# Two transformer blocks in one kernel: weight loads in another order beside a projection, SBUF tensors at other addresses

## What is computed

```python
# first block
proj = rmsnorm(h) @ w_in                       # q, k, v, gate of 8 retention heads, q, k, v of 8 forgetting heads
h = h + concat(silu(rg) * groupnorm(retention), forgetting_attention) @ w_out
h = h + softmax(q k / 16) v @ w_xo             # q = rmsnorm(h) @ w_xq; k, v from 256 memory rows @ w_xkv
h = h + (silu(hn @ w_gate) * (hn @ w_up)) @ w_down          # 1024 -> 2816 -> 1024
# second block, modulated by a condition c
sh1, sc1, g1, sh2, sc2, g2 = split(silu(c) @ w_ada + b_ada)  # six vectors of 1024
h = rmsnorm(x) * (1 + sc1) + sh1;  x = x + g1 * (concat(attention, pool_mixer) @ w_out)
h2 = rmsnorm(x) * (1 + sc2) + sh2; x = x + g2 * conv_gated_ffn(h2)   # 1024 -> 2 x 2816 -> 1024
```

## The kernel before

| tensors | before |
|---|---|
| h, xh, xl, raw, whi, wlo (every buffer) | 128 |
| tmp, rstd, region: fh, fl, xah, xal, memh, meml, qxh, expd, probt | 64 |
| adar 0 and 1, adacc | 64 |
| adar 2 and 3, adasum (they lie in xh and xl) | 128 |

## Time and profile before

### The profile page before, as it was taken

How to read it: one execution, slowest core, us unless ns; L and a number is a source line. 1 busy time by engine, 2 the same in 40 slices (tenths; PEclk the granted TensorE clock), 3 DMA queues, 4 the chain that set the end, 5 groups by cost and what they waited for, 6 DMA issues and landing times.

```text
span 1446.3 us, 17892 instructions
## 1 busy us (share of the span) xinstructions
PE 1387.2 (96%) x6616; PEld 1106.9 (77%) x6616; DVE 815.7 (56%) x1231; ACT 615.4 (43%) x851; POOL 613.0 (42%) x456
## 2 busy tenths in 40 slices
PE   5999999899989999999999889998999999999999
PEld 3777965788876888888888776874678888888887
DVE  6511957356433577777789994579355554553000
ACT  4634328553344443443441112478435455463111
POOL 4344420274430444445444444331244555556453
PEclk8999999999999999999999998999999999999999
DMA  6123112142220243433445552210121322232322
GB/s 258 59 89 114 58 58 88 41 143 109 88 87 1 88 151 144 156 131 131 147 160 207 206 196 102 88 59 30 59 88 58 109 94 87 92 111 87 117 87 87
DMA packets 28336, 154.19 MB, mean 107 GB/s; under 512 B 2944, under 2 KB 4096, under 8 KB 13952
## 3 DMA queue, kind: packets, MB, share of 16 engines
q1 hardware_dynamic: 28288, 153.52, 29.5%
HBM read 151.41 MB, written 2.10 MB: 106 GB/s over the span
## 4 chain that ended last, share of the span: by engine, by line
issue 42%; PE 30%; POOL 24%; DVE 3%; POOLq 0%; DMA 0%; ACT 0%; SPq 0%
POOL wlo L371 24%; PE lin L1318 10%; PE lin L1320 9%; PE lin L1319 9%; DVE small L984 1%; DVE expd L995 1%; PE lin L1512 0%; PE att L1374 0%; DMA h<-x_t 0%; DVE win L1208 0%; POOL tmp L364 0%; POOLq L365 0%; DVE small L988 0%; PE att L1389 0%; PE att L1383 0%
## 5 line engine op out<-in xcount | busy, mean ns | idle before, releaser
L371 POOL TENSOR_TENSOR wlo<-raw,whi 128x512 fp32r<-128x512 f32 x448 | 608.0, 1388 | 810.4 <-ACT whi L384 535.3
L1318 PE MATMUL lin<-xh,whi 128*128 128x512 f32 x1072 | 423.0, 395 | 4.3 <-POOL wlo L371 3.6
L1320 PE MATMUL lin<-xh,wlo 128*128 128x512 f32 x1072 | 418.1, 390 | 0.0
L1319 PE MATMUL lin<-xl,whi 128*128 128x512 f32 x1072 | 417.8, 390 | 0.0
L1318 PEld LDWEIGHTS lin<-xh,whi 128*128 128x128 f32 x1072 | 201.7, 188 | 51.8 <-issue 6.1
L1320 PEld LDWEIGHTS lin<-xh,wlo 128*128 128x128 f32 x1072 | 201.7, 188 | 42.8
L384 ACT ACTIVATE whi<-raw 128x2048 fp32r<-128x2048 f32 x67 | 128.4, 1917 | 247.8 <-PE lin L1320 211.2
L1319 PEld LDWEIGHTS lin<-xl,whi 128*128 128x128 f32 x1072 | 201.8, 188 | 41.1 <-issue 0.5
L1318 PE MATMUL lin<-fh,whi 128*128 128x512 f32 x352 | 142.2, 404 | 5.5 <-POOL wlo L371 5.5
L1319 PE MATMUL lin<-fl,whi 128*128 128x512 f32 x352 | 141.1, 401 | 0.0
L1320 PE MATMUL lin<-fh,wlo 128*128 128x512 f32 x352 | 140.9, 400 | 0.0
(11 more groups left out here) (292 smaller groups left out, 1961.8 us busy)
## 6 DMA issues: line engine op xcount, KB each, us to landing
raw<-w_slabs SPq DMA_DIRECT2D x112, 1024.0 KB, 4.8
adar<-ada SPq DMA_DIRECT2D x48, 512.0 KB, 3.3
h<-x_t SPq DMA_DIRECT2D x4, 512.0 KB, 7.1
decay<-decay SPq DMA_DIRECT2D x4, 512.0 KB, 8.6
out_t<-h SPq DMA_DIRECT2D x3, 512.0 KB, 8.2
rope<-rope SPq DMA_DIRECT2D x2, 512.0 KB, 8.1
memx<-mem_t SPq DMA_DIRECT2D x1, 1024.0 KB, 5.6
rcnt<-rcnt SPq DMA_DIRECT2D x4, 256.0 KB, 5.0
```

The lines of the kernel that those rows point to most:

```text
L371: last = nc.gpsimd.tensor_tensor(wlo[s][:, ks, :], raw[s][:, ks, :], f(whi[s][:, ks, :]), ALU.subtract)
L1318: nc.tensor.matmul(out, whi_, xhi_, start=first, stop=False)
L1319: nc.tensor.matmul(out, whi_, xlo_, start=False, stop=False)
L1320: return nc.tensor.matmul(out, wlo_, xhi_, start=False, stop=last)
```

## The change

It has two parts. The list in SP's order for the first down projection becomes (2, 3, 3, 3, 3, 3, 3, 2) where it was (4, 3, 3, 3, 3, 3, 2, 1), 22 tiles in both. And the tensors are placed otherwise: par, mod, small, cact, warm and convp come first, then h at the next multiple of 2048 with xh, xl and raw behind it, then the weight buffers with bytes of their own added to them, then rstd, tmp and region, and con between region and tail.

| tensors | after, modulo 256 |
|---|---|
| h, xh, xl, raw (also 0 modulo 2048) | 0 |
| whi 0, whi 1, wlo 0, wlo 1 | 32, 96, 160, 224 |
| rstd, tmp, region: fh, fl, xah, xal, memh, meml, qxh, expd, probt, and con | 0 |
| adar 0 and 1, adacc | 64 |
| adar 2 and 3, adasum | 0 |

```diff
--- before.py
+++ after.py
@@ -103,6 +103,14 @@
             return {n: sem(f"{prefix}_{n}") for n in names.split()}
 
 
+        par = sb("par", [P, PARAMS["end"]])
+        mod = sb("mod", [P, MODS])
+        small = sb("small", [P, 64])
+        cact = sb("cact", [P, KT])
+        warm = sb("warm", [P, 1])
+        convp = [sb(f"convp{i}", [P, 8]) for i in range(2)]
+        at[0] = -(-at[0] // 2048) * 2048
+
         h = sb("h", [P, KT, T])
         xh_at = at[0]
         xh = sb("xh", [P, KT, T], F32R)
@@ -111,20 +119,18 @@
 
         ret_raw = sb("ret_raw", [P, 4, T], offset=xl_at)
         raw = [sb(f"raw{i}", [P, KT, COLS]) for i in range(2)]
-        whi = [sb(f"whi{i}", [P, KT, COLS], F32R) for i in range(2)]
-        wlo = [sb(f"wlo{i}", [P, KT, COLS], F32R) for i in range(2)]
-        par = sb("par", [P, PARAMS["end"]])
-        con = sb("con", [P, CONSTS["end"]])
-        mod = sb("mod", [P, MODS])
-        small = sb("small", [P, 64])
-        cact = sb("cact", [P, KT])
-        warm = sb("warm", [P, 1])
-        convp = [sb(f"convp{i}", [P, 8]) for i in range(2)]
+        wh_at = at[0]
+        at[0] += 4 * 4 * KT * COLS
+        wl_at = wh_at + 2 * 4 * KT * COLS
+        whi = [sb(f"whi{i}", [P, KT, COLS], F32R, offset=wh_at + i * 4 * KT * COLS + (32, 96)[i]) for i in range(2)]
+        wlo = [sb(f"wlo{i}", [P, KT, COLS], F32R, offset=wl_at + i * 4 * KT * COLS + (160, 224)[i]) for i in range(2)]
+        at[0] += 256
         rstd = sb("rstd", [P, T])
         tmp_at = at[0]
         tmp = [sb(f"tmp{i}", [P, T]) for i in range(4)]
         region = at[0]
         at[0] += 88 * 1024
+        con = sb("con", [P, CONSTS["end"]])
         tail = at[0]
 
         def rg_sb(name, shape, kib, dt=F32):
@@ -326,7 +332,7 @@
                 load_ada(j, j - FT)
 
             j = FT + 4
-            for u, more in enumerate((4, 3, 3, 3, 3, 3, 2, 1)):
+            for u, more in enumerate((2, 3, 3, 3, 3, 3, 3, 2)):
                 for _ in range(more):
                     sp.wait_ge(ada["acc"], j - 3)
                     load_ada(j, (j - FT) % 4)
```

## The result

| | before | after |
|---|---|---|
| median of 4 runs, us | 1449.74 | 1463.65 |
| lowest, highest | 1448.65, 1450.37 | 1460.12, 1465.28 |
| the profiled execution | 1448.1 | 1465.28 |
| its span | 1446.3 | 1463.5 |

The ratio is 1.009, with a 95% interval from 1.0076 to 1.0105: 13.9 us slower. The forecast was 1415 us. The time lies in the range, near its upper end, and on the other side of no change.

What follows compares the result with a forecast made beforehand. TensorE's (PE's) matmul steps were taken as the bound; savings of 19.2 (xh), 13.3 (fh, xah) and 2.6 us (mix_tm), 35.1 in sum, took 1448.1 to 1413.0, plus 2.0 for the median: 1415 us. Own range 1402 to 1435, whole 1390 to 1470.

Steps and rivals of the forecast that it cites:

- The reading of the rows: On PE: the next weight load and running stream meet in SBUF, as addresses and relative timing set; 6.7 to 20.0 ns overhead.
- The order edit: First down projection: value 0, ±3.7 us, since VectorE's unbroken chain bounds it; PE's slab 7 gain is lost at the last modulation.
- Rival 5: First down projection: if VectorE's chain weren't the bound, 5.5 us of waits and cold starts would go, some 8 us less; no chance given.
- Addresses outside PE: On VectorE, ScalarE and GpSimd: new addresses cost 0; a tenth more on ScalarE or GpSimd would hide.
- The step that failed: On PE: the smallest overhead in any row, 6.7 ns from memk, taken for all products, 35.1 us less in sum.
- the term of xh: 2880 matmuls with xh as moving operand: step goes to 220.0 ns, 6.67 ns less each, 19.2 us less.
- that of fh and xah: 996 matmuls with fh or xah as moving operand: 13.3 ns less each, 13.3 us less.
- rival 4: 512-column xh products, ffn stages above all: equal residues were the good case, 233.3 ns everywhere, slower, 1468 us; chance 0.21.
- Rival 1: PE's products: the conflict goes altogether, steps of 213.3 ns, 63.4 us less, 1387 us; chance 0.19.
- Rival 2: PE's products: only the odd tensors (fh, xah) are mended, all at 226.7 ns, 6.6 us less, 1443 us; chance 0.14.
- Rival 3: PE's products: nothing changes; region or buffer differs and addresses don't count, or gains and losses cancel, 1450 us; chance 0.13.
- Signs named beforehand: Profile signs of error: steps above 228 ns, even and odd slabs differing, longer ScalarE or GpSimd instructions, gaps in VectorE's chain.

Runs made afterwards that it cites:

- equal: The kernel before with 64 bytes left free ahead of rstd, so rstd, tmp and region start at 128 like the weights: 1443.87 us against 1450.25.
- map1: Not the kernel: 52 series of 48 fp32r matmuls with chosen start addresses, PE alone at work; 512-column steps 226.7 to 234.4 ns.
- map2: Not the kernel: 45 series of 48 matmuls, varying distance, width, what stands ahead, and patterns of weight tensors; 512-column steps 226.7 to 233.4 ns.
- short_steps: The kernel before with the multiply-adds of VectorE's 26 modulation steps cut from 128 columns to 16: 1434.35 us against 1450.61.
- weights_back: The changed kernel with the four weight buffer offsets set to 0, so streams, region and weights all start at 0: 1443.73 us (before 1448.76).

## Why the prediction was wrong

- **What bounds the kernel** was right: PE's step sets the time, outside the first down projection. The counts held too: 2880, 996 and 384 times the change of their steps give 14.1 us where 13.9 were measured, and 996 × 6.7 ns = 6.6 us stands against the 6.4 us that equal gains. That the first two come within 0.2 us of each other is partly luck, since ffn and ffn2 grow by 0.9 and 1.5 us less than their count.
- **The reading of the rows** was right in its first half: the addresses of the two operands set the step (map1). Their relative timing, the second half, does so too: with 256 columns at one distance (map2), and with 512 only in the changed kernel's mixture (231.2 and 233.2 ns at the same addresses in ffn2), by 2 ns.
- **The order edit** at 0 was right, and so was the reason: VectorE's chain (short_steps: 16.3 us). The place was wrong. What PE gains at slab 7 (3.57 us) is waited for at slab 8 (5.25 where it was 0.15), not at the last modulation, whose wait is 2.52 us in both. The load left 5.6 us earlier, not 8. Rival 5, by which the order would count, falls with it.
- **Addresses outside PE** at 0 were right: in the changed kernel a free modulation step still takes 2.68 us, whi's copy by ScalarE 1.92 us, GpSimd's part of a slab 5.2 to 5.4 in ffn.
- **The step that failed** is "I take the smallest overhead that a row shows, 6.7 ns, for all". By it the 512-column step would be 220.0 ns; the changed kernel has 231.2 to 233.4, an overhead of 18 to 20 ns over 213.3. So the term of xh, 19.2 us less in the forecast, came out as 15.8 us more, and that of fh and xah as 1.1 us less in place of 13.3. The 6.7 came from memk's third slab in the earlier trace rows, a product of 256 columns (weights stationary, distance 64). map2 has both of memk's steps, 113.3 and 117.8, at this distance and the same addresses: the row was a state of timing and no property of unequal residues. Nor could it speak for 512 columns. The 256-column steps of the earlier trace rows and the 512-column ones of the earlier trace rows already showed that the order of good and bad turns round between the two widths. For 512 columns there were two rows, equal residues 226.7 and unequal ones 233.3, and the change took equality from 2880 products. The reading nearest to the rows was rival 4.
- **Rival 4** was right in its mechanism and its place. It was too high by 4.4 us (1468 against 1463.65), in the main because it put all steps at 233.3. Most of the even slabs outside ffn2, those with weights at 32 and 160, have 231.2.
- **The other rivals.** Rival 1 needed steps of 213.3, and no fp32r series came under 226.7. Rival 2 (all at 226.7) is what equal and weights_back are, not the change. Rival 3, by which addresses count for nothing, falls with equal and weights_back: two other sets of addresses in the same regions and buffers gave 226.7 for fh. It leaned on the Trainium skill, "SBUF — State Buffer", Who interferes with whom, by which TensorE never waits on anyone. Of other engines no run speaks against that: the kernel's steps of 226.7 and 233.3 are those of PE alone. For bfloat16 the addresses count for nothing as well (215.8 ns at every distance, close to the 215.7 of the Trainium skill, "TensorE: Matmul & The Clock Gate", Part 1). For fp32r they do count: 226.7 to 234.4 ns by distance alone, with nothing else at work.
- **Signs named beforehand.** "Steps above 228 ns" and "steps that differ between even and odd slabs" both appeared. The mixture is the two triples of map2. The other two, longer instructions on ScalarE or GpSimd and gaps in VectorE's chain, did not: it is busy for 106.5 of its 113.0 us.

Open remains what inside SBUF or PE makes the distance count, and why it does so modulo 256. The runs fix the dependence: fp32r, not bfloat16; 512 columns best at distance 0. They don't show its cause, nor what puts the slabs with weights at 32 and 160 at one or the other of their two steps.

## What to carry to other kernels

For fp32r products of 512 columns, place every stationary and moving tensor at one residue modulo 256; here that alone gave 6.4 us of 1450 with one line, and breaking it cost 14. When two rows of the product that sets the time contradict the smallest row of another shape, the forecast goes by the two. And before an earlier load is valued, ask which chain ends the stage: cut that chain in a trial, and see whether the order matters with it or without it.

## What the runs showed that I had not expected

- The step of an fp32r 128x512 product depends on the distance of the two starts down to four bytes (232.5 ns against 226.7), and repeats with 256 bytes.
- It isn't symmetric: 192 (64 below) takes 228.9 ns, 64 above 233.3.
- 256-column products at distance 64 have two steady states, 113.3 and 117.8 ns, chosen by what stands ahead of them. With 512 columns two weight tensors at 32 and 224 in turn take 230.0 ns, where each alone takes 233.3.
- 504 columns take as long as 512 (226.7 ns both); at 496, distance 0 takes 223.4 and distance 64 only 220.0; 448 columns at distance 0 took 206.7 in one series and 202.7 in another.
- A modulation step of seven instructions beside GpSimd's subtraction takes 6.42 us with 128 columns and 5.82 with 16: the slowing hardly depends on the size of the instruction.
